# Moving the start addresses of weight tiles in SBUF: F panels by 64 bytes, down and gate panels by a table

## The chip, the cores and the metric

One core of one Trainium2 chip runs the whole kernel in one launch. The metric is the device time in microseconds of one execution. Of the kernel before there are three runs: 1002.62, 1002.34 and 1002.54 us, median 1002.54.

## The reference, cut to what matters

The reference takes x (256 tokens by 1024 features, float32) through two layers of one kind and then a block of another kind. Only the chain of products matters here; each has 1024 input features unless noted.

```
layer 0: h = x + mixer_ab(rmsnorm(x))           # stick-breaking attention and a gated recurrence, 3584 + 1024 columns
layer 1: h = h + mixer_c(rmsnorm(h))            # sliding-window attention, 1536 + 1024 columns
both:    h = h + conv_glu_ffn(rmsnorm(h))       # up 5632 columns, 3-tap convolution, silu(gate)*up, down 2816 -> 1024
         h = h + sigmoid(rmsnorm(h) @ ple_gate) * (p @ ple_proj)
block 2: proj = rmsnorm(h) @ w_in               # 9472 columns: three branches and three mixing gates
         y = sum over branches of (branch @ w_branch) * sigmoid(gate)
         out = rmsnorm(h + y @ w_out)
```

All products are of float32 data.

## The kernel before, in words

**Splitting.** TensorE is used in its float32r mode. Each operand is split in a high part (rounded to float32r) and a low part (the rest), and each product is three matmuls: high by high, high by low, low by high. The activations are in x_hi and x_lo or y_hi and y_lo (8 tiles of 128 features by 256 tokens each), in g_hi and g_lo (the FFN's gated features, and the branch outputs in block 2) or in pt_hi and pt_lo.

**Panels.** All weights are cut into 157 panels of 128 x 2048 floats (1 MB), in a fixed order (`PANELS`). SyncE loads panel n into one of three raw slots; ScalarE makes `w_hi` of it (L1211), VectorE makes `w_lo` (L1539, one panel is made by GpSimd, L734), both in rings of three slots (L369, L370); then TensorE multiplies. A load waits until `w_lo` of the panel three before is made (L632), and ScalarE waits until TensorE is done with the panel three before.

**Three kinds of panel**, each with its own order of matmuls in TensorE's function `panel`:
- F (67 panels, 48 matmuls each, L866): the weights are the operand that is loaded into the array (128 x 128) and the activations are streamed (256 columns). These are the two FFN up products (22 panels each: up0 with y, up1 with x), and fb, qb, qa, ka, mk, qc, gc, ga, gb2 and ub (23 panels, all with x).
- W (58 panels, 24 matmuls each, L841): the activations are loaded (128 x 128) and the weights are streamed (512 columns). Fourteen of them use y: kv, qs, wo1 and gate1. The mixing gates of block 2 are mc, mb and ma, four panels each.
- BT (32 panels, 24 matmuls each, L898, or L886 for the last panel of a branch): activations loaded, weights streamed (512 columns), four results at once. These are the FFN's down products (down0 and down1, 11 panels each), pp0, pp1 and the branch products brc, brb, bra.

TensorE loads the operand of the next matmul while the present one is streaming: in the trace each LDWEIGHTS begins together with the matmul before the one it is for.

**Addresses.** Tensors are placed by hand, in bytes of a partition. The first one is at 16512, that is 128 modulo 256. The `fixed` tensors (the raw, high and low slots, x_hi, x_lo, h, xn, whose place y_hi shares, ident, tri, vecs, small, g_hi and g_lo) follow each other in sizes that are multiples of 256 bytes; a slot of weights is 8192 bytes. Behind them, in regions that several stages share, come the others. All sizes there are multiples of 256 bytes but that of `relb` (32 x 16 floats, 64 bytes), which stands ahead of `buck`, y_lo and row_early (L435 to L438). So all operands of the products begin at 128 modulo 256 and y_lo begins at 192. Steps inside a tensor are 512, 1024, 2048 or 4096 bytes.

**Order.** All engines walk one list of steps, `SCHEDULE`, built by `schedule()`; each engine does its part of a step and waits on semaphores for the rest. Between the panels stand the attention steps, the turns (transposes) and, in up0 after its sixth panel, the small matmul of the bias step (L1073).

## Time and profile before

| | |
|---|---|
| median of three runs | 1002.54 us (1002.34 to 1002.62) |
| the profiled execution's own time | 1002.47 us |
| its span, first to last instruction | 1000.4 us |
| PE busy | 982.3 us, 98% (6186 matmuls) |
| PEld (weight loads) busy | 880.0 us, 88% |
| DVE / ACT / POOL busy | 674.2 / 573.8 / 135.9 us |
| mean granted clock of TensorE | 0.998 of full speed |
| DMA | 173.65 MB, mean 174 GB/s |

A matmul's recorded duration overlaps the next one's, so the durations say little of the pace. The pace is the distance from one start to the next: the time of a piece of the chain divided by its count of matmuls, or the difference of two starts in the timeline divided by the number of matmuls between them. The timeline rounds starts to 0.01 us.

### The profile page before, as it was taken

Reading aid. Unit: us, or ns where it says so; the run is one execution under the profiler, and the core shown is the slowest. Engines: PE = TensorE matmul, PEld = TensorE weight load, DVE = VectorE, ACT = ScalarE, POOL = GpSimd, SP = SyncE. Lnnn points to the kernel's source line nnn. Section 1 sums busy time; section 2 is a strip of 40 time slices with the busy share of each in tenths; the row PEclk is TensorE's granted clock in tenths of the full one; section 3 lists DMA queues with packets and bytes.
Section 4 is the critical chain, followed back from the end, with each engine's and each line's share of the span. In section 5 each row is a group of like instructions: output and inputs, shape, how many; then the busy total and the mean of one; then the engine's idle time right before and its main releaser. Section 6 shows DMA issues by size and latency. Waiting matters only on the chain.

```text
span 1000.4 us, 15440 instructions
## 1 busy us (share of the span) xinstructions
PE 982.3 (98%) x6186; PEld 880.0 (88%) x6186; DVE 674.2 (67%) x963; ACT 573.8 (57%) x801; POOL 135.9 (14%) x119
## 2 busy tenths in 40 slices
PE   8999999999999999999999999999999999999997
PEld 8988889999988888788999998888988889988886
DVE  5886477888863567876788886456564566854555
ACT  7747747566543576775756654356464465534433
POOL 5002202343310000000133331001000000000010
PEclk9999999999999999999999999999999999999999
DMA  9654266687555555336666655546645544456541
GB/s 295 199 168 126 85 166 178 194 245 200 173 208 178 163 206 169 127 116 170 188 171 191 187 172 208 175 161 206 211 128 169 168 155 140 146 192 209 175 170 55
DMA packets 159510, 173.65 MB, mean 174 GB/s; under 512 B 4110, under 2 KB 120320, under 8 KB 159440
## 3 DMA queue, kind: packets, MB, share of 16 engines
q1 hardware_dynamic: 157104, 167.00, 53.3%
q0 software_dynamic: 2160, 5.41, 1.7%
q8 instruction: 49, 0.80, 0.3%
q10 hardware_dynamic: 176, 0.27, 0.1%
q14 instruction: 21, 0.17, 0.1%
HBM read 171.59 MB, written 1.07 MB: 173 GB/s over the span
## 4 chain that ended last, share of the span: by engine, by line
PE 82%; DVE 7%; ACT 6%; issue 3%; DMA 1%; SPq 0%; POOL 0%; POOLq 0%; ACTq 0%; DVEq 0%
PE bank L866 31%; PE bank L841 28%; PE bank L898 16%; ACT w_hi L1211 2%; DVE w_lo L1539 2%; PE bank L886 2%; PE bank L926 1%; PE bank L1000 1%; ACT le L1321 1%; DMA w_raw<-in_ab_w_in 1%; DMA h<-in_x 1%; ACT L1321 1%; PE bank L946 0%; DVE x_lo L1553 0%; DVE le_s L1901 0%
## 5 line engine op out<-in xcount | busy, mean ns | idle before, releaser
L1539 DVE TENSOR_TENSOR w_lo<-w_raw,w_hi 128x2048 fp32r<-128x2048 f32 x154 | 352.0, 2289 | 188.6 <-ACT w_hi L1211 188.5
L1211 ACT ACTIVATE w_hi<-w_raw 128x2048 fp32r<-128x2048 f32 x155 | 296.2, 1914 | 243.4 <-PE bank L866 113.5
L866 PE MATMUL bank<-x_hi,w_hi 128*128 128x256 f32 x720 | 205.9, 286 | 0.8 <-DVE w_lo L1539 0.5
L866 PE MATMUL bank<-x_hi,w_lo 128*128 128x256 f32 x720 | 203.7, 283 | 0.0
L866 PE MATMUL bank<-x_lo,w_hi 128*128 128x256 f32 x720 | 203.7, 283 | 0.0
L841 PE MATMUL bank<-w_hi,x_hi 128*128 128x512 f32 x352 | 140.2, 398 | 3.2 <-DVE kaT L1695 2.2
L866 PEld LDWEIGHTS bank<-x_hi,w_hi 128*128 128x128 f32 x720 | 138.0, 192 | 2.4 <-DVE w_lo L1539 0.7
L866 PEld LDWEIGHTS bank<-x_lo,w_hi 128*128 128x128 f32 x720 | 138.1, 192 | 0.2
L866 PEld LDWEIGHTS bank<-x_hi,w_lo 128*128 128x128 f32 x720 | 138.0, 192 | 0.0
L841 PE MATMUL bank<-w_hi,x_lo 128*128 128x512 f32 x352 | 137.8, 391 | 0.0
L841 PE MATMUL bank<-w_lo,x_hi 128*128 128x512 f32 x352 | 137.6, 391 | 0.0
L694 POOL TENSOR_TENSOR gf<-sgate,cc 128x256 f32<-128x256 f32 x44 | 82.2, 1869 | 161.5 <-ACT sgate L1238 161.5
L866 PE MATMUL bank<-y_hi,w_hi 128*128 128x256 f32 x352 | 98.8, 281 | 0.1
L866 PE MATMUL bank<-y_hi,w_lo 128*128 128x256 f32 x352 | 98.4, 280 | 0.0
L866 PE MATMUL bank<-y_lo,w_hi 128*128 128x256 f32 x352 | 98.4, 279 | 0.0
L841 PEld LDWEIGHTS bank<-w_hi,x_hi 128*128 128x128 f32 x352 | 66.2, 188 | 18.2 <-DVE kaT L1695 2.6
L841 PEld LDWEIGHTS bank<-w_hi,x_lo 128*128 128x128 f32 x352 | 66.4, 189 | 14.2
L841 PEld LDWEIGHTS bank<-w_lo,x_hi 128*128 128x128 f32 x352 | 66.5, 189 | 13.2
L1648 DVE SCALAR_TENSOR_TENSOR cc<-conv_in,vecs,cc 128x254 f32<-128x254 f32 (+1 forms) x176 | 73.9, 482 | 0.0
L898 PE MATMUL bank<-w_hi,g_hi 128*128 128x512 f32 x216 | 66.7, 390 | 0.0
L898 PE MATMUL bank<-w_hi,g_lo 128*128 128x512 f32 x216 | 66.5, 389 | 0.0
L898 PE MATMUL bank<-w_lo,g_hi 128*128 128x512 f32 x216 | 66.5, 389 | 0.0
(353 smaller groups left out, 1461.4 us busy)
## 6 DMA issues: line engine op xcount, KB each, us to landing
w_raw<-in_ffn_up SPq DMA_DIRECT2D x88, 512.0 KB, 5.2
w_raw<-in_w_in SPq DMA_DIRECT2D x35, 1024.0 KB, 5.1
w_raw<-in_ffn_down SPq DMA_DIRECT2D x22, 1024.0 KB, 4.9
w_raw<-in_ab_w_in SPq DMA_DIRECT2D x13, 1024.0 KB, 5.2
w_raw<-in_ple_gate SPq DMA_DIRECT2D x8, 1024.0 KB, 5.1
w_raw<-in_c_w_in SPq DMA_DIRECT2D x6, 1024.0 KB, 5.4
w_raw<-in_ab_w_out SPq DMA_DIRECT2D x4, 1024.0 KB, 5.1
w_raw<-in_w_mem_kv SPq DMA_DIRECT2D x4, 1024.0 KB, 5.8
```

The lines of the kernel that those rows point to most:

```text
L694: pool.tensor_tensor(gf[i % 2][:, :], sgate[i % 2][:, :], cc[i % 3][:, 1, :], ALU.mult).then_inc(*mark("gated", ("gf", l, i)))
L841: mm = pe.matmul(bank[b][:, :], x[:, 4 * half + k, t * P:(t + 1) * P], wv[w][:, k, :], start=(half == 0 and k == 0 and m == 0), stop=(half ...
L866: mm = pe.matmul(bank[b][:, c * 256:c * 256 + 256], wv[w][:, k, c * P:(c + 1) * P], x[:, k, :], start=(k == 0 and m == 0 and not (first an ...
L886: mm = pe.matmul(bank[out_bank(t, half)][:, :], x[:, k0 + 2 * i + k, t * P:(t + 1) * P], wv[w][:, k, half * 512:half * 512 + 512], start=F ...
L898: mm = pe.matmul(bank[out_bank(t, half)][:, :], x[:, k0 + 2 * i + k, t * P:(t + 1) * P], wv[w][:, k, half * 512:half * 512 + 512], start=( ...
L926: mm = pe.transpose(bank[b][:, q * 256 + t * P:q * 256 + (t + 1) * P], src[:, t, kt * P:(kt + 1) * P], ident[:, :])
L1000: mm = pe.matmul(bank[b][:, o:o + 64], X[:, hd, t * P:(t + 1) * P], later(X[:, hd:hd + 1, t * P:(t + 1) * P], LEVELS[li])[:, 0, :, :], sta ...
L1211: act.activation(whi[n % RING][:, :], raw[n % RAW][:, :], ACT.Copy).then_inc(*mark("weights_hi", ("hi", n)))
L1321: act.activation(dst, src, ACT.Exp, scale=scale, bias=s_neg[:, c:c + 1], accum_out=s_sum[:, c:c + 1]).then_inc(*mark("exponentials", ("e", ...
L1539: dve.tensor_tensor(wlo[n % RING][:, :], raw[n % RAW][:, :], plain(whi[n % RING][:, :]), ALU.subtract).then_inc(*mark("weights_lo", ("lo", ...
L1648: dve.scalar_tensor_tensor(v, conv_ins[int(stage[-1])][i % 2][:, c, 0:T - d], vec("ffn_conv", int(stage[-1]), tap)(c * FT + i), v, ALU.mul ...
```

## The change

The high and low slots become 64 floats (256 bytes) longer, and a panel's weights begin `shift_of(n)` floats into its slot, the same in the high and the low slot, whichever of the three it is: 16 floats (64 bytes) for every F panel; for down and gate panels what a table says; 0 for all others. In the table the down products have one value for each group of three panels, and the two last panels of each product have 0.

| panels | bytes |
|---|---|
| down0, panels 0-2 / 3-5 / 6-8 | 16 / 32 / 48 |
| down1, panels 0-2 / 3-5 / 6-8 | 192 / 128 / 64 |
| mc / mb / ma, four panels each | 96 / 112 / 80 |

Beside that the region's next address is rounded so that y_lo begins at 128 modulo 256 like the others. To make room, `tri` moves from the fixed tensors to a region of the first layer, and `causal` to a part of `vecs` that held convolution weights. The raw slots stay where they are relative to each other. No instruction is added or removed.

```diff
--- before.py
+++ after.py
@@ -31,6 +31,8 @@
 FOURS = len(LEVELS)
 ORDER = [-1, FOURS] + list(range(FOURS))
 RAW, RING = 3, 3
+ROOM, F_SHIFT = 64, 16
+W_SHIFT = {("down0", 0): 4, ("down0", 1): 8, ("down0", 2): 12, ("down1", 0): 48, ("down1", 1): 32, ("down1", 2): 16, "mc": 24, "mb": 28, "ma": 20}
 WARM_UP = 12
 BIAS_AT = 6
 PIECES = {0: 4, 1: 2}
@@ -194,6 +196,12 @@
 def block_done(stage, block):
 
     return FIRST[stage] + (2 + block if stage in HALVES_FIRST else 2 * block + 1)
+
+
+def shift_of(n):
+
+    stage, i, _, kind, _ = PANELS[n]
+    return F_SHIFT if kind == "F" else W_SHIFT.get((stage, i // 3), 0) if kind == "BT" else W_SHIFT.get(stage, 0)
 
 
 WIDE_BLOCK = {}
@@ -366,14 +374,22 @@
             return t
 
         raw = [fixed(f"w_raw{i}", [P, 2048]) for i in range(RAW)]
-        whi = [fixed(f"w_hi{i}", [P, 2048], F32R) for i in range(RING)]
-        wlo = [fixed(f"w_lo{i}", [P, 2048], F32R) for i in range(RING)]
+        hi_room = [fixed(f"w_hi{i}", [P, 2048 + ROOM], F32R) for i in range(RING)]
+        lo_room = [fixed(f"w_lo{i}", [P, 2048 + ROOM], F32R) for i in range(RING)]
+
+        def w_hi(n):
+            a = shift_of(n)
+            return hi_room[n % RING][:, a:a + 2048]
+
+        def w_lo(n):
+            a = shift_of(n)
+            return lo_room[n % RING][:, a:a + 2048]
+
         XH, XL = (fixed(n, [P, KT, T], F32R) for n in ("x_hi", "x_lo"))
         h = fixed("h", [P, TT, D])
         xn_at = top[0]
         xn = fixed("xn", [P, TT, D])
         ident = fixed("ident", [P, P])
-        tri = fixed("tri", [P, P])
         vecs = fixed("vecs", [P, 5, P])
         small = fixed("small", [P, 320])
         g_at = top[0]
@@ -406,7 +422,7 @@
         sc_in, sc_over = g("sc_in", [P, HG_HEADS * TT, P]), g("sc_over", [P, HG_HEADS, P])
         exb = g("exb", [P, HG_HEADS, T])
         xs_buf = [r(f"xs{i}", [P, HG_HEADS, T]) for i in range(2)]
-        ones = g("ones", [P, P])
+        ones, tri = g("ones", [P, P]), r("tri", [P, P])
         heads = lambda x: x.rearrange("p (h t) -> p h t", h=HG_HEADS)
         four_q, four_k = heads(prod[:, :, :].rearrange("p t c -> p (t c)")), heads(on[:, :, :, :].rearrange("p t h c -> p (t h c)"))
         four_mid = prod[:, 0, 0:T].rearrange("p (n a) -> p n a", a=1)
@@ -433,6 +449,7 @@
         bias = r("bias", [P, SW_HEADS, T])
         brow = r("brow", [16, 3 * P])
         relb, buck = r("relb", [32, 16]), r("buck", [32, P])
+        r.at += (t_at - r.at) % 256
         YL = r("y_lo", [P, KT, T], F32R)
         YH = nc.alloc_sbuf_tensor_at("y_hi", [P, KT, T], F32R, offset=xn_at)
         row_early = r("row_early", [P, T])
@@ -463,7 +480,6 @@
         le, wT = r("le", [P, 2, 2, T]), r("wT", [P, 2, 2, T])
         va2, vb = r("va2", [P, TT, 768]), r("vb", [P, TT, 768])
         wsp, bsp = r("wsp", [P, GROUPS, P]), r("bsp", [P, GROUPS, P])
-        causal = r("causal", [P, T])
         r = Region(t_at, t_at + 4 * 3072)
         ubs, ga = r("ubs", [P, GROUPS, T]), r("ga", [P, MOBA_HEADS, T])
         r = Region(t_at + 4 * 3072, end)
@@ -502,6 +518,7 @@
         sw_tmp = [qkn[:, 0, 23, :], qkn[:, 0, 15, :]]
 
         vflat = vecs[:, :, :].rearrange("p a b -> p (a b)")
+        causal = vflat[:, 3 * P:3 * P + T]
 
         def vec(name, layer, *more):
             return lambda i: vflat[:, VEC[(name, layer, *more)] + i:VEC[(name, layer, *more)] + i + 1]
@@ -731,7 +748,7 @@
                     n = args[0]
                     pool.wait_ge(*at(("hi", n)))
                     for c in (slice(512 * q, 512 * q + 512) for q in range(4)):
-                        pool.tensor_tensor(wlo[n % RING][:, c], raw[n % RAW][:, c], plain(whi[n % RING][:, c]), ALU.subtract).then_inc(*mark("weights_lo_p", ("lo", n)))
+                        pool.tensor_tensor(w_lo(n)[:, c], raw[n % RAW][:, c], plain(w_hi(n)[:, c]), ALU.subtract).then_inc(*mark("weights_lo_p", ("lo", n)))
                 elif kind == "sb_scores":
                     i = args[0]
                     for r in range(2):
@@ -770,7 +787,7 @@
                     load(wsp_raw, io["w_spatial_2"][0].rearrange("g t s -> t g s"), "wsp")
                     load(bsp[:, :, :].rearrange("p g t -> p (g t)"),
                          bass.AP(tensor=io["b_spatial_2"].tensor, offset=0, ap=[[0, P], [1, GROUPS * P]]), "bsp")
-                    load(causal[:, :], io["c_causal"], "causal")
+                    load(causal, io["c_causal"], "causal")
                     load(small[:, 0:64], io["c_rope"], "rope")
                     pool.wait_ge(*at(("loaded", "wsp")))
                     pool.affine_select(out=wsp_raw, in_=wsp_raw, compare_op=ALU.is_ge, fill=0.0, base=0, pattern=[[0, GROUPS], [-1, P]], channel_multiplier=1).then_inc(*mark("spatial_masked", ("wspm",)))
@@ -808,7 +825,7 @@
 
                 stage, i, name, kind, where = PANELS[n]
                 xh, xl, k0, needs = XIN[stage]
-                wh, wl = whi[n % RING], wlo[n % RING]
+                wh, wl = w_hi(n), w_lo(n)
                 pieces = PIECES.get(n, 1)
                 pe.wait_ge(*at(("lo_piece", n, 0) if pieces > 1 else ("lo", n)))
 
@@ -825,7 +842,7 @@
                             turn(k, j)
                 if kind == "W":
                     block, half = where[2:]
-                    wv = [w[:, :].rearrange("p (k n) -> p k n", k=4) for w in (wh, wl)]
+                    wv = [w.rearrange("p (k n) -> p k n", k=4) for w in (wh, wl)]
                     for t in range(TT):
                         b = wide_bank(stage, block, t)
                         if half == 0:
@@ -849,7 +866,7 @@
                 elif kind == "F":
                     b = pb(n)
                     claim(b, ("ev", n))
-                    wv = [w[:, :].rearrange("p (k n) -> p k n", k=KT) for w in (wh, wl)]
+                    wv = [w.rearrange("p (k n) -> p k n", k=KT) for w in (wh, wl)]
                     first = i == 0
                     for c, k in [(c, k) for k in range(KT) for c in range(2)] if first else [(c, k) for c in range(2) for k in range(KT)]:
                         if c == 0 and first:
@@ -877,7 +894,7 @@
                         for t in range(TT):
                             for half in range(2):
                                 claim(out_bank(t, half), ("h", stage, t) if down else ("ym", stage[-1], 2 * t + half) if branch else ("ev", FIRST["gate" + stage[-1]] + 2 * half + 1))
-                    wv = [w[:, :].rearrange("p (k n) -> p k n", k=2) for w in (wh, wl)]
+                    wv = [w.rearrange("p (k n) -> p k n", k=2) for w in (wh, wl)]
                     if branch and last:
 
                         for t, half in [(t, half) for t in range(TT) for half in range(2)]:
@@ -1208,13 +1225,13 @@
                     act.wait_ge(*at(("raw", n)))
                     if n >= RING:
                         act.wait_ge(*at(("pe", n - RING)))
-                    act.activation(whi[n % RING][:, :], raw[n % RAW][:, :], ACT.Copy).then_inc(*mark("weights_hi", ("hi", n)))
+                    act.activation(w_hi(n), raw[n % RAW][:, :], ACT.Copy).then_inc(*mark("weights_hi", ("hi", n)))
 
             def split_piece(n, i):
 
                 c = slice(2048 // PIECES[n] * i, 2048 // PIECES[n] * (i + 1))
                 act.wait_ge(*at(("raw_half", i // 2) if n == 0 else ("raw", n)))
-                act.activation(whi[n % RING][:, c], raw[n % RAW][:, c], ACT.Copy).then_inc(*mark("weights_hi", ("hi_piece", n, i)))
+                act.activation(w_hi(n)[:, c], raw[n % RAW][:, c], ACT.Copy).then_inc(*mark("weights_hi", ("hi_piece", n, i)))
 
             act.dma_start(xn[0:2 * KT, 0, 0:P], io["mix_norm"].rearrange("l (a c) -> (l a) c", c=P)).then_inc(*mark("load_mix_gain", ("loaded", "mix_gain"), by=16))
 
@@ -1536,13 +1553,13 @@
             def split(n):
                 if n < len(PANELS) and n != POOL_SPLIT:
                     dve.wait_ge(*at(("hi", n)))
-                    dve.tensor_tensor(wlo[n % RING][:, :], raw[n % RAW][:, :], plain(whi[n % RING][:, :]), ALU.subtract).then_inc(*mark("weights_lo", ("lo", n)))
+                    dve.tensor_tensor(w_lo(n), raw[n % RAW][:, :], plain(w_hi(n)), ALU.subtract).then_inc(*mark("weights_lo", ("lo", n)))
 
             def split_piece(n, i):
 
                 c = slice(2048 // PIECES[n] * i, 2048 // PIECES[n] * (i + 1))
                 dve.wait_ge(*at(("hi_piece", n, i)))
-                dve.tensor_tensor(wlo[n % RING][:, c], raw[n % RAW][:, c], plain(whi[n % RING][:, c]), ALU.subtract).then_inc(*mark("weights_lo", ("lo_piece", n, i), ("lo", n)))
+                dve.tensor_tensor(w_lo(n)[:, c], raw[n % RAW][:, c], plain(w_hi(n)[:, c]), ALU.subtract).then_inc(*mark("weights_lo", ("lo_piece", n, i), ("lo", n)))
 
             def rest(src, gain, hi, lo, name, event, *first):
```

## Rows read from the trace of the kernel before

**Rows 1.** The page: busy shares, granted clock in 40 slices, the chain that ended last.
```profile
PE 982.3 (98%) x6186; PEld 880.0 (88%) x6186; DVE 674.2 (67%) x963; ACT 573.8 (57%) x801; POOL 135.9 (14%) x119
...
PEclk9999999999999999999999999999999999999999
...
PE 82%; DVE 7%; ACT 6%; issue 3%; DMA 1%; SPq 0%; POOL 0%; POOLq 0%; ACTq 0%; DVEq 0%
PE bank L866 31%; PE bank L841 28%; PE bank L898 16%; ACT w_hi L1211 2%; DVE w_lo L1539 2%; PE bank L886 2%; PE bank L926 1%; PE bank L1000 1%; ACT le L1321 1%; DMA w_raw<-in_ab_w_in 1%; DMA h<-in_x 1%; ACT L1321 1%; PE bank L946 0%; DVE x_lo L1553 0%; DVE le_s L1901 0%
```
**Rows 2.** The chain in order of time: start us, us, engine, output, line, count.
```profile
155.35 28.05 PE bank L866 x234
183.72 90.66 PE bank L866 x768
...
452.29 5.54 PE bank L841 x24
...
479.34 120.22 PE bank L866 x1002
600.00 65.31 PE bank L898 x288
...
894.34 21.76 PE bank L841 x96
```
**Rows 3.** Timeline of PE, first and second FFN: start us, us, instruction.
```profile
183.12 0.28 PE L866 MATMUL bank<-y_hi,w_lo 128*128 128x256 f32 x1
183.33 0.39 PE L1073 MATMUL bank<-buck,relb 32*16 32x128 f32 x2
...
249.84 0.28 PE L866 MATMUL bank<-y_hi,w_hi 128*128 128x256 f32 x1
...
250.90 0.28 PE L866 MATMUL bank<-y_hi,w_hi 128*128 128x256 f32 x1
...
539.76 0.28 PE L866 MATMUL bank<-x_lo,w_hi 128*128 128x256 f32 x1
...
540.84 0.28 PE L866 MATMUL bank<-x_lo,w_hi 128*128 128x256 f32 x1
```
**Rows 4.** Timeline of PE in the second PLE gate, the first and nineteenth start.
```profile
674.09 0.39 PE L841 MATMUL bank<-w_hi,y_hi 128*128 128x512 f32 x1
...
678.25 0.39 PE L841 MATMUL bank<-w_hi,y_hi 128*128 128x512 f32 x1
```
**Rows 5.** Tiles y_lo and w_lo: durations ns min/median/max, and who waited for w_lo.
```profile
L841 PE MATMUL bank<-w_hi,y_lo x112: 389/397/398, 365.8 to 690.7; 128*128 128x512 f32 x112
...
L1539 DVE TENSOR_TENSOR w_lo<-w_raw,w_hi x154: 2277/2291/2295, 19.1 to 980.0; 128x2048 fp32r<-128x2048 f32 x154
...
  PEld bank L866: 1.1, 2
  PE bank L866: 0.7, 2
```
**Rows 6.** Groups of PE by line and form: count, busy us, mean ns.
```profile
L866 PE MATMUL bank<-x_hi,w_hi 128*128 128x256 f32 x720 | 205.9, 286 | 0.8 <-DVE w_lo L1539 0.5 <-DVE w_lo L1545 0.2
...
L841 PE MATMUL bank<-w_hi,x_lo 128*128 128x512 f32 x352 | 137.8, 391 | 0.0
...
L866 PE MATMUL bank<-y_hi,w_hi 128*128 128x256 f32 x352 | 98.8, 281 | 0.1
...
L841 PE MATMUL bank<-w_hi,y_hi 128*128 128x512 f32 x112 | 44.6, 398 | 0.7 <-DVE y_lo L1553 0.7
```
**Rows 7.** Busy time of each engine in a stretch of the second FFN.
```profile
core 0: us, PE busy (x) PEld busy (x) DVE busy (x) ACT busy (x) POOL busy (x), PEclk, DMA share, GB/s
480.00:590.00 110.00, 110.00 (x919) 110.00 (x918) 90.95 (x132) 68.75 (x95) 35.35 (x18) 1.00 0.66 187
```
**Rows 8.** The page's DMA issues: count, KB each, us to landing.
```profile
w_raw<-in_ffn_up SPq DMA_DIRECT2D x88, 512.0 KB, 5.2
w_raw<-in_w_in SPq DMA_DIRECT2D x35, 1024.0 KB, 5.1
```

## The prediction

> **What bounds the kernel now.** First the page's busy shares and the granted clock: PE is busy 98% of the span, the next engine (DVE) 67%, and the clock stands at its upper level, 2.4 GHz, in all 40 slices [rows 1]. Then the chain that ended last: 82% PE, and three lines of weight products (L866, L841, L898) hold 75% of it [rows 1]. So the time is the number of matmuls times the distance from one start to the next; waits can give little. The distances come from the chain in order of time [rows 2]. L866 in the second FFN: 120.22 us for 1002 matmuls, 120.0 ns each. L898: 65.31/288 = 226.8. L841 in the last wide stages: 21.76/96 = 226.7. From 256 to 512 streamed columns the distance grows by 106.7 ns, 0.417 ns a column, one cycle at 2.4 GHz. What is left is 13.3 ns (32 cycles), the same for both widths. I call it the fixed part; 32 cycles on each matmul is what the change can reach.
>
> **Why addresses may matter.** All weight slots and all activations of the products start at the same place modulo 256 bytes, but for one buffer: `relb` has 64 bytes a partition, so y_lo, allocated behind it, lies 64 bytes further. That gives two natural experiments.
> - y_lo streamed (first FFN, L866, weights loaded). After 184 us, 90.66/768 = 118.0 ns [rows 2]; a look at ten starts gives 1.06/9 = 117.8 against 1.08/9 = 120.0 in the second FFN [rows 3]. Only one matmul in three streams y_lo, so three of them cost 353.3 instead of 360: 6.7 ns, 16 cycles. Before 183.3 us the same stage runs at 28.05/234 = 119.9 [rows 2], and it changes over just where one small matmul of the bias step stands between panels [rows 3]: the gain depends on how the streams were in step before.
> - y_lo loaded (wide stages of the sliding attention and second PLE gate, L841, weights streamed). 4.16/18 = 231.1 ns [rows 4], and 5.54/24 = 230.8 in a panel of the output product [rows 2], against 226.7: three cost 13.3 ns (32 cycles) more. The durations say the same, 397 ns where y_lo is the loaded operand [rows 5] against a mean of 391 for x_lo [rows 6].
>
> So the addresses of the two operands do change the distance, and with both signs.
>
> **The change, part by part.** No instruction, DMA or wait is added or taken; starts of tensors move. The tables `tri` and `causal` go to other places, loaded by the same DMAs at the same points of their queues, behind the same waits: nothing.
>
> *F panels, x inputs.* 720 x 3 = 2160 matmuls [rows 6] load weights that now lie 64 bytes after the streamed input. Not shown before: this pair in every matmul. From above the nearest row is the loaded y_lo, +13.3 ns a load; from below the whole fixed part, -13.3 ns. I take the streamed y_lo, since line, shape and stage kind are the same: one offset pair saves 6.7 ns and the two equal ones nothing. With all three offset it is 6.7 ns each: 113.3 ns. 2160 x 6.67 = -14.4 us. I choose this against the sign: there the streamed operand was the one further on, here the loaded one is, as in the L841 stages. My reason is that equal starts carry the fixed part everywhere (120.0, 226.7, 226.8), which looks like a collision at the moment when load and stream begin together, while in the L841 stages the loaded base also jumps from matmul to matmul, which the new layout doesn't do.
>
> *F panels, y inputs.* 352 x 3 = 1056 matmuls [rows 6] of the first FFN, now (234 x 119.9 + 768 x 118.0)/1002 = 118.5 ns. y_lo is aligned and the weights are offset, so 113.3: 1056 x 5.2 = -5.5 us.
>
> *y_lo aligned in the wide stages.* 112 x 3 = 336 matmuls [rows 6] get the addresses of the x stages: 231.1 to 226.7, 336 x 4.4 = -1.5 us. This term is the surest.
>
> *The table.* 18 down and 12 gate panels, 24 matmuls each: 720, all streaming the shifted weights. Six panels (64 and 192 bytes, 144 matmuls) are like the streamed y_lo: -6.7 ns, -1.0 us. The other 24 (16, 32, 48, 80, 96, 112, 128 bytes) have no row near them; I take zero. Bounds for all 720: the fixed part gone or doubled, 9.6 us either way.
>
> *Cover.* If a panel of the FFN takes 48 x 113.3 = 5.44 us instead of 5.76, DVE's 90.95 us in 110 [rows 7] becomes 88% of the time, and ACT's 68.75 66%: they still fit. The split of a panel takes DVE 2.29 us [rows 5], and PE waited for it 1.8 us in all [rows 5]. A panel's load lands 5.2 us after issue [rows 8] with three raw slots. What would be late next is DVE, from about 100 ns a matmul. Shifted writes of ACT and DVE I cost at nothing: they lie beside PE.
>
> **Sum.** -14.4 - 5.5 - 1.5 - 1.0 = -22.4 us, against the profiled execution's 1002.47 us (span 1000.4 and 2.07 around it): 980.1. The median of the runs is 0.07 us higher, no difference here. I forecast 980.
>
> The skill bears on this against the change. The Trainium skill, TensorE: Matmul & The Clock Gate, section on the steps of a matmul, says that PE reads the streamed operand and the loaded one through two independent ports, and that loading "doesn't steal SBUF read bandwidth from the running matmul". By that no start address would matter, and the sum would be zero; the trace disagrees, with 117.8 and 120.0, and 231.1 and 226.7, for the same work. That is the third rival below. The same page's section on the issue gap has N/2.4 + 2.5 ns, 109.2 for 256 columns, where the row has 120.0; an estimate by it would put the floor at 968 us.
>
> **The rivals.**
> 1. *The sign decides (slower).* Loaded 64 bytes after streamed costs 13.3 ns, as the wide y stages show, and now every F matmul has that pair: 133.3 ns. 2160 x 13.3 = +28.8, 1056 x (133.3 - 118.5) = +15.6, less 1.5: 1045. For it: it is the only row with this sign. Against: that row has jumping bases and 512 columns. The point from which it decides: any F distance above 120.3 ns makes the kernel slower.
> 2. *Small gain.* An offset anywhere only brings the pace of the settled first FFN, 117.8 to 118.0: 2160 x 2.1 = -4.5, 1056 x 0.6 = -0.6, less 1.5, table about 0: 996. For it: it is what a row shows outright.
> 3. *Nothing.* F stays at or returns to 120.0: 1056 x 1.5 = +1.6, -1.5: 1002.6. Ports that don't collide would give this.
> 4. *The table costs.* F as in 3, and starts that are no multiple of 64 bytes cost 6.7 to 13.3 ns on 720 matmuls: +4.8 to +9.6, 1007 to 1012.
> 5. *The whole fixed part of F goes.* -13.3 x 2160 - 11.8 x 1056 - 1.5 us: 960.
>
> **How the numbers follow.** Forecast (about 980, with the table's bounds 970 to 990) 0.38; small gain 0.22; all of it gone 0.03; nothing 0.08; the table costs 0.12; the sign decides 0.17. A measurement of this kernel can tell about 0.2%, 2 us, from no change. Faster: 0.38 + 0.22 + 0.03 = 0.63; same 0.08; slower 0.12 + 0.17 = 0.29. The range leaves out 960 and 1045, 0.20 together: from 970 (forecast with the table at its best bound) to 1013 (nothing in F, the table at its worst). The forecast's own range is 970 to 990.
>
> **What would show it.** L866 distances in the second FFN: 113.3 (forecast), 117.8 (rival 2), 120.0 (3), 133.3 (1). L841 in the y stages: 226.7, and the 397 ns of y_lo down to 389 to 391. The down panels fall into three groups of three, each with its own distance, beside two unshifted ones at 226.7; likewise the gate panels of the last block. DVE's and ACT's busy time should stay within 1%. I am wrong if F goes above 120.3 ns, if the distance follows the sign and not the offset, or if PE begins to wait for w_lo.

## The result and the profile after

The kernel after takes 994.39 us (median; 993.91 to 999.28) where the kernel before, on the same chips, takes 1002.30: a ratio of 0.9931, interval 0.9915 to 0.9948. It is faster by 8 us, where 22 had been forecast.

The profiled execution of after is the longest of its seven, 999.28 us; the other six lie between 993.91 and 994.85. So the profile shows 3.2 of those 8 us, and the other 5 need an explanation of their own (they get one below). Lines have moved: L866 is now L883, L841 is L858, L898 is L915.

The page of after: busy time, granted clock, and the chain that ended last, by line.

```profile
PE 978.4 (98%) x6186; PEld 873.8 (88%) x6186; DVE 674.4 (68%) x963; ACT 573.8 (58%) x801; POOL 134.0 (13%) x119
...
PEclk9999999999999999999999999999999999999999
...
PE bank L883 30%; PE bank L858 28%; PE bank L915 16%; PE bank L903 2%; DVE w_lo L1556 2%; ACT w_hi L1228 2%; PE bank L943 1%; PE bank L1017 1%; DMA w_raw<-in_ab_w_in 1%; ACT le L1338 1%; ACT L1338 1%; PE bank L963 0%; DVE x_lo L1570 0%; PE bank L986 0%; DVE le_s L1918 0%
```

Against [rows 1] nothing has changed place: PE is busy 98% of the span, the clock is at its upper level in all 40 slices (one dip of a few us doesn't show in them; it is told of at the end), and three lines of weight products hold 74% of the chain. DVE (674.4 us) and ACT (573.8 us) are busy as long as before. So the difference again lies in the distance from one matmul to the next.

The chain of after in order of time (start us, us, engine, output, line, count):

```profile
154.41 26.55 PE bank L883 x234
181.28 90.66 PE bank L883 x768
272.38 66.65 PE bank L915 x288
...
477.62 118.02 PE bank L883 x1002
596.08 66.46 PE bank L915 x288
...
837.31 16.96 PE bank L883 x144
856.96 22.42 PE bank L858 x96
...
890.30 22.18 PE bank L858 x96
...
928.84 22.19 PE bank L858 x96
```

Divide each by its count. First FFN: 113.5 ns up to the bias step, then 118.0; before, 119.9 and 118.0 [rows 2]. Second FFN: 118.02/1002 = 117.8 ns (120.0 before). The three ub panels (837.31): 117.8. Down products: 66.65/288 = 231.4 and 66.46/288 = 230.8 ns, 226.8 before [rows 2]. Mixing gates mc, mb, ma: 22.42, 22.18 and 22.19 us for 96, that is 233.5, 231.0 and 231.1 ns, 21.76 (226.7) for mb before [rows 2]. One product became faster, the other slower.

Two starts nine matmuls apart, in the timeline of PE in the first FFN, ahead of the bias step and behind it:

```profile
169.92 0.28 PE L883 MATMUL bank<-y_hi,w_hi 128*128 128x256 f32 x1
...
170.94 0.28 PE L883 MATMUL bank<-y_hi,w_hi 128*128 128x256 f32 x1
...
249.87 0.28 PE L883 MATMUL bank<-y_hi,w_hi 128*128 128x256 f32 x1
...
250.93 0.28 PE L883 MATMUL bank<-y_hi,w_hi 128*128 128x256 f32 x1
```

1.02/9 = 113.3 ns and 1.06/9 = 117.8 ns: the same instructions on the same addresses at two paces. Panel by panel (the median of the sums of three distances, a third of it) every F panel of after runs at one of these two, 13 of the 67 at 113.3 to 114.7 and 54 at 117.7 to 118.0.

The tile y_lo of after as the loaded operand (count, ns min/median/max):

```profile
L858 PE MATMUL bank<-w_hi,y_lo x112: 388/389/398, 364.7 to 687.5; 128*128 128x512 f32 x112
```

Who waited for w_lo in after (us, times):

```profile
  PE bank L883: 2.0, 1
```

y_lo's products take 389 ns, where [rows 5] had 397. PE's wait for w_lo rose from 0.7 to 2.0 us.

**What the profiled execution adds up to.** First FFN -1.5 us (117.21 for 118.71), second FFN -2.2, wide stages with y -1.2 (four stages, the sum of their distances), the table +3.9 (down 1.34 + 1.15, gates 0.6 + 0.4 + 0.4), the 15 F panels of layer 1 and the last block -2.3, the start up to the first FFN -0.9 (155.35 to 154.41). That is -4.2; the span went down by 3.1, so 1.1 us more went into pauses that I didn't follow. The 0.9 us of the start needn't be F's pace alone: a short dip of the clock lies elsewhere in the two executions (last section).

### The profile page after: what moved, and what is told of

It reads as the page before. It is cut to its first block, busy times and chain, and to the rows that moved or that the text cites. A ratio compares the mean times of both kernels' runs of the same rounds, so it can differ in the third digit from the quotient of the medians.

```text
span 997.3 us, 15440 instructions
## 1 busy us (share of the span) xinstructions
PE 978.4 (98%) x6186; PEld 873.8 (88%) x6186; DVE 674.4 (68%) x963; ACT 573.8 (58%) x801; POOL 134.0 (13%) x119
## 4 chain that ended last, share of the span: by engine, by line
PE 83%; DVE 7%; ACT 6%; issue 3%; DMA 1%; POOL 0%; POOLq 0%; ACTq 0%; DVEq 0%
PE bank L883 30%; PE bank L858 28%; PE bank L915 16%; PE bank L903 2%; DVE w_lo L1556 2%; ACT w_hi L1228 2%; PE bank L943 1%; PE bank L1017 1%; DMA w_raw<-in_ab_w_in 1%; ACT le L1338 1%; ACT L1338 1%; PE bank L963 0%; DVE x_lo L1570 0%; PE bank L986 0%; DVE le_s L1918 0%
## 5 line engine op out<-in xcount | busy, mean ns | idle before, releaser
L883 PE MATMUL bank<-x_hi,w_hi 128*128 128x256 f32 x720 | 204.8, 284 | 2.1 <-DVE w_lo L1556 2.0
L883 PE MATMUL bank<-x_lo,w_hi 128*128 128x256 f32 x720 | 202.4, 281 | 0.0
L883 PE MATMUL bank<-x_hi,w_lo 128*128 128x256 f32 x720 | 202.4, 281 | 0.0
L858 PE MATMUL bank<-w_hi,x_hi 128*128 128x512 f32 x352 | 140.1, 398 | 2.6 <-DVE kaT L1712 1.5
L883 PEld LDWEIGHTS bank<-x_hi,w_hi 128*128 128x128 f32 x720 | 136.3, 189 | 3.7 <-DVE w_lo L1556 2.2
L858 PE MATMUL bank<-w_lo,x_hi 128*128 128x512 f32 x352 | 137.7, 391 | 0.0
L883 PEld LDWEIGHTS bank<-x_hi,w_lo 128*128 128x128 f32 x720 | 137.6, 191 | 0.0
L858 PE MATMUL bank<-w_hi,x_lo 128*128 128x512 f32 x352 | 137.5, 391 | 0.0
L883 PEld LDWEIGHTS bank<-x_lo,w_hi 128*128 128x128 f32 x720 | 136.4, 189 | 0.2
L883 PE MATMUL bank<-y_hi,w_hi 128*128 128x256 f32 x352 | 98.9, 281 | 0.1
L883 PE MATMUL bank<-y_lo,w_hi 128*128 128x256 f32 x352 | 98.5, 280 | 0.0
L883 PE MATMUL bank<-y_hi,w_lo 128*128 128x256 f32 x352 | 98.5, 280 | 0.0
L858 PEld LDWEIGHTS bank<-w_hi,x_hi 128*128 128x128 f32 x352 | 66.1, 188 | 18.2 <-DVE kaT L1712 2.0
L858 PEld LDWEIGHTS bank<-w_hi,x_lo 128*128 128x128 f32 x352 | 66.0, 188 | 14.5
L858 PEld LDWEIGHTS bank<-w_lo,x_hi 128*128 128x128 f32 x352 | 66.1, 188 | 13.4
L883 PEld LDWEIGHTS bank<-y_hi,w_hi 128*128 128x128 f32 x352 | 67.2, 191 | 0.5 <-DVE y_lo L1570 0.3
L915 PE MATMUL bank<-w_hi,g_hi 128*128 128x512 f32 x216 | 67.5, 394 | 0.0
L915 PE MATMUL bank<-w_lo,g_hi 128*128 128x512 f32 x216 | 67.4, 393 | 0.0
```

The lines of the kernel that those rows point to most:

```text
L858: mm = pe.matmul(bank[b][:, :], x[:, 4 * half + k, t * P:(t + 1) * P], wv[w][:, k, :], start=(half == 0 and k == 0 and m == 0), stop=(half ...
L883: mm = pe.matmul(bank[b][:, c * 256:c * 256 + 256], wv[w][:, k, c * P:(c + 1) * P], x[:, k, :], start=(k == 0 and m == 0 and not (first an ...
L915: mm = pe.matmul(bank[out_bank(t, half)][:, :], x[:, k0 + 2 * i + k, t * P:(t + 1) * P], wv[w][:, k, half * 512:half * 512 + 512], start=( ...
```

## The experiments

Each kernel is the kernel after with the edit that is shown, unless the text says otherwise.

| kernel | what it is | us, median | ratio to before |
|---|---|---|---|
| f_only | F 64 bytes, no table | 991.39 (991.06 to 992.42) | 0.9894 (0.9879 to 0.9909) |
| y_only | only y_lo aligned | 1003.12 (1001.51 to 1003.86) | 1.0010 (1.0001 to 1.0019) |
| f_minus | F 192 bytes, no table | 993.27 (988.15 to 994.07) | 0.9895 (0.9865 to 0.9925) |
| base_plus | f_only, all tensors 64 bytes on | 991.77 | one run |
| after_again | the kernel after, once more | 993.88 | one run |
| f_kick | f_only, three panels at 80 bytes | 994.21 (992.04 to 994.56) | 0.9917 (0.9903 to 0.9930) |
| bias_late | f_only, bias step later | 989.51 | one run |
| scan | a start of its own for each panel | 1000.58 | one run |
| scan_fine | the same, near 64 and 192 bytes | 997.26 | one run |
| f_52 | F 52 bytes, no table | 987.78 (986.55 to 988.69) | 0.9853 (0.9840 to 0.9867) |
| f_76 | F 76 bytes, no table | 1000.47 (998.89 to 1000.89) | 0.9979 (0.9970 to 0.9988) |
| f_mix | F 52 or 76 bytes by stage | 985.28 (984.98 to 986.97) | 0.9843 (0.9828 to 0.9858) |
| halves | f_only, gates in matmuls of 256 | 992.87 | one run |

### The parts of the change

**f_only**: F panels at 64 bytes, the table empty.

```diff
-W_SHIFT = {("down0", 0): 4, ("down0", 1): 8, ("down0", 2): 12, ("down1", 0): 48, ("down1", 1): 32, ("down1", 2): 16, "mc": 24, "mb": 28, "ma": 20}
+W_SHIFT = {}
```

> Only the F panels are offset (64 bytes); the table is empty, y_lo is aligned. Theory: the table only costs. In the changed kernel's profile its 720 matmuls run at 228.9 to 233.3 ns instead of 226.7, some 3.9 us in all, so this version takes about 990.5 us, with all down and mixing-gate panels back at 226.7 ns. F panels run at one of two paces, 113.3 or 117.8 ns, changing only at pauses. Rival (the table's groups were harmless and their longer distances come from elsewhere, such as the slower writes of ScalarE): 994 us and L915 still above 226.7.

The chain of f_only:

```profile
154.26 27.56 PE bank L883 x234
182.14 87.27 PE bank L883 x768
269.85 65.33 PE bank L915 x288
...
473.76 118.02 PE bank L883 x1002
592.22 65.32 PE bank L915 x288
...
851.94 21.81 PE bank L858 x96
```

Both down products are back at 226.8 ns, and mc (851.94) is at 227.2. The median is 3.0 us below that of after, against the 3.9 us of the table's pieces. So the table only cost. The F pieces show something else: here the first FFN is slow up to the bias step (27.56/234 = 117.8) and fast behind it (87.27/768 = 113.6), the reverse of after.

**y_only**: neither F nor the table shifted; only y_lo lies like the others.

```diff
-ROOM, F_SHIFT = 64, 16
+ROOM, F_SHIFT = 64, 0
```

with `W_SHIFT = {}` as above.

> Only y_lo is aligned; all weights start at 0. Theory (relative start decides): wide y stages at 226.7 instead of 231.1 (-1.5 us), first FFN at 120.0 instead of 118.5 (+1.6 us), so 1002 to 1003 us. Rival (aligning alone gives part of the gain): 1000 us or below, with F under 120 ns.

```profile
154.52 28.06 PE bank L883 x234
182.90 92.35 PE bank L883 x768
...
479.75 120.22 PE bank L883 x1002
```

That is the chain of y_only: 119.9, 120.2 and 120.0 ns. With all starts equal every F panel runs at 120.0, also behind the bias step, where [rows 2] had 118.0: +1.7 us, which takes away what the wide stages with y gained. The gain of the change comes from F's offset, 991.39 - 1003.12 = -11.7 us, against which stand the table's 3.0 us and the 0.8 of y_only (1003.12 - 1002.30). The three add up to the 7.9 us of the change by the way they are formed; the sum is no test of its own.

### Is it the sign, or the place in memory?

**f_minus**: F panels 192 bytes in, which is 64 bytes ahead of the next streamed start modulo 256.

```diff
-ROOM, F_SHIFT = 64, 16
+ROOM, F_SHIFT = 64, 48
```

with `W_SHIFT = {}`.

> F panels' weights 192 bytes in, that is 64 bytes behind the streamed input instead of ahead, no table, y_lo aligned. Theory A (only that the two starts differ by 64 bytes counts, not which is ahead): same paces as with 64 bytes, 990 to 992 us. Theory B (the sign counts, as streamed and loaded operand are not alike): other paces; the streamed y_lo of before, the only row with this sign, saved 16 cycles in one of three, so 113.3 ns throughout and 983 to 985 us if each offset pair saves as much, or up to 120 ns and 1002 us if not.

The same two paces as in f_only, 113.3 (18 panels) and 117.8 (49), and 993.27 us. The sign doesn't decide. That 192 bytes ahead is the same as 64 behind takes a period of 256 bytes for granted; no run tests it by itself, but the slots are 8448 bytes long, so their starts alternate modulo 512, and the paces don't alternate from panel to panel. Its executions spread over 6 us (988.15 to 994.07), more than those of any other kernel here.

**base_plus**: f_only with every tensor that is placed by hand 64 bytes further on.

```diff
-        top = [16512]
+        top = [16576]
```

> The version with only the F panels offset, but all tensors of the kernel begin 64 bytes later (the first at 16576 instead of 16512). Theory (only the difference between the streamed and the loaded operand's start counts): W and BT panels at 226.7 ns, F at 113.3 or 117.8, 988 to 993 us. Rival (the place itself counts, modulo 256): other distances, F back at 120.0 or W and BT above 226.7.

991.77 us, the F panels again at 113.3 and 117.8 only, the down panels and mixing gates at 226.7. So what counts is how the starts stand to each other, not where they are, as far as one shift of 64 bytes shows it.

### The two rhythms

**after_again**: the kernel after, unchanged.

> The changed kernel once more, unchanged. Its profiled run took 999.3 us and its other six 994.3. Theory (two rhythms, fixed anew at the pauses): the time difference of one execution to the next lies in F panels alone, in whole stretches at 113.3 or 117.8 ns; if this execution takes about 994 us, some 20 more panels run at 113.3 ns than in the first profile. Rival (the 5 us come from elsewhere, such as the clock or DMA): the same paces in each F panel as in the first profile, and longer waits.

The chain of after_again:

```profile
180.65 90.66 PE bank L883 x768
...
476.68 113.59 PE bank L883 x1002
```

113.59 us for the second FFN, where the profiled execution of after has 118.02, with the same program. These 4.4 us are most of the 5.4 between the two executions (993.88 and 999.28). So an execution can take one of two rhythms in a stage and stays in it for over a thousand matmuls: 113.4 ns (with the pauses between panels) or 117.8.

**f_kick**: three single panels at 80 bytes, to see whether another offset throws PE out of its rhythm.

```diff
+KICK = {("up0", 1): 20, ("up0", 7): 20, ("up1", 2): 20}
...
-    return F_SHIFT if kind == "F" else W_SHIFT.get((stage, i // 3), 0) if kind == "BT" else W_SHIFT.get(stage, 0)
+    return KICK.get((stage, i), F_SHIFT) if kind == "F" else 0
```

> The version with only the F panels offset, but one panel early in each FFN's up product (the second and, behind the bias matmul, the eighth of the first FFN, the third of the second FFN) lies 80 bytes in. In the run in which every panel had its own start, all four panels at 64 bytes that were entered from another offset, without a pause, ran at 113.3 ns. Theory (two rhythms for the same addresses, kept until something breaks step; a panel at another offset brings PE into the fast one): both up products run at 113.3 ns behind these panels; against the version without them that saves 0.9 us (four panels before the bias matmul) + 4.1 us (19 panels of the second FFN) and costs 0.8 us: 987 us. Rival (the rhythm is a matter of chance at every change): no difference beyond 1 us from 991.4, and the two stages at 117.8 or 113.3 as it falls.

```profile
182.39 90.71 PE bank L884 x768
...
477.19 113.86 PE bank L884 x1002
```

That is its chain. The shifted panel itself goes at 118.7 ns, and after it the rhythm is the one from before: slow in the first FFN (90.71/768 = 118.1, where after_again without a shifted panel has 90.66), fast in the second (113.86 against 113.59; 48 x 5.4 ns = 0.26 for the one panel). Panel 1 of up0 says nothing: behind panel 0 the pace changes in after_again too. The theory that a panel at another offset brings PE into the fast rhythm fell, with its 987 us; the median is 994.21, 2.8 us above f_only's, and the profiled execution, 992.04, doesn't show why.

**bias_late**: the small matmul of the bias step comes after panel 14 instead of 6.

```diff
-BIAS_AT = 6
+BIAS_AT = 14
```

with `W_SHIFT = {}`.

> 64 bytes as before, but the bias matmul stands behind 14 panels of the first FFN instead of 6. In each of six profiles the first FFN's rhythm changed just at this matmul. Theory (a rhythm is kept until something breaks step): the first FFN changes its pace, if at all, at panel 14 and no more at panel 6. Rival (the pace depends on the panel or on what the other engines do then): it changes at panel 6 again.

```profile
154.94 70.07 PE bank L883 x618
225.32 45.44 PE bank L883 x384
...
475.03 113.59 PE bank L883 x1002
```

The chain of bias_late: 70.07/618 = 113.4 ns up to the step at its new place, 45.44/384 = 118.3 behind it. The change of pace moved with the foreign matmul. In the kernels in which all F panels have the same start the rhythm changes inside an FFN at two places only, at that matmul and behind the first panel, where PE pauses; elsewhere it may be another behind each pause of PE. What a pause or a foreign matmul does to it isn't in the program's hands as far as these runs go.

### The other offsets

**scan** and **scan_fine**: each panel of the FFNs (in scan those of the mixing gates too) has a start of its own.

```diff
-    return F_SHIFT if kind == "F" else W_SHIFT.get((stage, i // 3), 0) if kind == "BT" else W_SHIFT.get(stage, 0)
+    return SCAN[stage][i] if stage in SCAN else F_SHIFT if kind == "F" else 0
```

> Every panel of both FFN up products, both down products and the mixing gates has a start of its own: up0 and up1 take 0 to 240 bytes in steps of 16 in two different orders, with a few starts of 4, 8, 68, 72 and 132 bytes; the down and gate panels 4 to 248 bytes. The time says nothing, the distance within each panel does. Theory A (the difference modulo 256 bytes counts in 64-byte blocks): paces of F fall into plateaus of 64 bytes with 0 the slowest at 120.0, and for the streamed weights 0 is the best at 226.7 ns. Theory B (any difference will do): every F panel but 0 runs at 113 to 118 ns. Rival C (starts off a 64-byte boundary cost an extra line): 16, 32 and 48 bytes are slower than 0 in F too, as they were in the down panels (232 to 233 ns).

The timeline of scan in the second FFN: first and last start of 48 steps in the panel at 64 bytes, then the same in the panel at 112 bytes.

```profile
494.78 0.28 PE L889 MATMUL bank<-x_hi,w_hi 128*128 128x256 f32 x1
...
500.23 0.28 PE L889 MATMUL bank<-x_hi,w_hi 128*128 128x256 f32 x1
...
511.63 0.28 PE L889 MATMUL bank<-x_hi,w_hi 128*128 128x256 f32 x1
...
517.39 0.28 PE L889 MATMUL bank<-x_hi,w_hi 128*128 128x256 f32 x1
```

5.45/48 = 113.5 ns and 5.76/48 = 120.0 ns. Read so, panel by panel (ns; more values where more panels had the offset):

| bytes modulo 256 | F, weights loaded, 256 columns streamed | down and gates, weights streamed, 512 columns |
|---|---|---|
| 0 | 120.0 | 226.7 |
| 4 / 8 / 12 | 118.3 / 115.6, 115.8 / 116.6 | 8: 233 |
| 16 / 32 / 48 | 118.4 / 118.3 / 117.8 | 231.6 / 233 / 230 to 233 |
| 20 / 24 / 28 / 36 / 40 / 44 | 120.0 / 122.0 / 116.8 / 120.0 / 119.3 / 118.0 | not tried |
| 52 / 56, 60 | 113.3, 113.3 / 117.8, 119.6 | not tried |
| 64 | 113.3 or 117.7 | 229 |
| 68, 72 | 118.3 | not tried |
| 76 / 80 | 113.3 / 118.7 | 80: 231 |
| 96 | 117.3, 118.8, 120.1 | 233.3 |
| 112 / 128 | 120.0 / 118.8 | 231.1 / 232.2 |
| 132 to 176 | 118.2 to 120.0 | 233 to 234 |
| 180 to 188 / 196 to 204 / 212, 216 | 118.0 to 118.4 / 116.7 to 120.0 / 117.4, 119.8 | not tried |
| 192 | 113.3 or 117.8 | 233.4 |
| 208 / 224 | 116.7 / 116.7, 117.8 | 234.5 / 233 |
| 240 / 248 | 119.8 / not tried | 236.5 / 235.4 |

Two results. Offsets in F are no worse than equal starts, with one exception of size (24 bytes, 122 ns), and only 52, 64, 76 and 192 bytes reached 113.3. At 96 and 224 bytes, too, panels differ in pace. For streamed weights equal starts are the best of all; each of the 17 other starts costs 2.2 to 9.8 ns.

> Each panel of the two up products with a start of its own again, now in steps of 4 bytes around 64 and 192 and below 64. Theory (64 and 192 are sharp best points, 16 cycles above the streaming time at 113.3 ns): every start 4 bytes beside them is slower, 115 to 119 ns, as 68 and 72 bytes were (118.3). Rival (the 115.8 ns at 8 bytes shows a second valley): some start between 4 and 60 bytes comes to 113.3 ns or below. The panels at 64 and 192 bytes, entered from another offset, run at 113.3 in most cases.

scan_fine found the fast pace at 52 bytes (two panels of two) and at 76 (one of one), while 64 had it once and the slow one twice, and 192 once and three times the slow one. In scan the four panels at 64 that were entered from another offset without a pause had all been fast. So in these two runs panels with the same start go at both paces within one FFN, with only other offsets between them: a stretch of other offsets can change the rhythm as well, though f_kick's single panels didn't. That asked for whole kernels.

**f_52** and **f_76**: all F panels at one of the two.

```diff
-ROOM, F_SHIFT = 64, 16
+ROOM, F_SHIFT = 64, 13
```

(19 in f_76), with `W_SHIFT = {}`.

> F panels' weights 52 bytes in instead of 64, nothing else. In the finer run both panels at 52 bytes ran at 113.3 ns, one in each FFN, while panels at 64 did so in one of three. Theory (at 52 bytes there is only the fast rhythm): all F panels at 113.3 to 113.5 ns; against the 992.4 us of the profiled execution with 64 bytes, where 41 panels ran at 117.8, 41 x 48 x 4.4 ns = 8.7 us less, 984 us, and executions within 0.5 us of each other. Rival (52 bytes has two rhythms as well, and was lucky twice): 991 us with a spread of several us and stretches at a slower pace.

> F panels' weights 76 bytes in. One panel at 76 bytes ran at 113.3 ns. Theory (52 and 76, 12 bytes to either side of 64, behave alike): all F panels at 113.3 ns, 984 us. Rival (one panel of luck): 990 us or more, with panels at 117.8 to 119 ns.

The chain of f_52:

```profile
182.16 87.25 PE bank L883 x768
...
473.49 113.61 PE bank L883 x1002
...
827.66 17.29 PE bank L883 x144
```

and that of f_76:

```profile
183.45 92.36 PE bank L883 x768
...
479.86 120.24 PE bank L883 x1002
...
840.92 16.35 PE bank L883 x144
```

Both theories (984 us, all panels fast) fell: f_52 takes 987.78 us and f_76 1000.47. These offsets too have two rhythms, 113.3 and 120.0. They fall otherwise: f_52 is fast in both FFNs (113.6, 113.4) and slow in ten other panels (the ub ones, 17.29/144 = 120.1); f_76 is slow in both FFNs (120.3, 120.0) and in the first three F panels of the last block, and fast in its last ten (the ub ones, 16.35/144 = 113.5).

**f_mix**: for each stage the offset that had been fast in it.

```diff
-ROOM, F_SHIFT = 64, 16
+ROOM, F_SHIFT = 64, 19
+W_SHIFT = {}
+F_STAGE = {"up0": 13, "up1": 13, "mk": 13, "qc": 13, "gc": 13}
...
-    return F_SHIFT if kind == "F" else W_SHIFT.get((stage, i // 3), 0) if kind == "BT" else W_SHIFT.get(stage, 0)
+    return F_STAGE.get(stage, F_SHIFT) if kind == "F" else 0
```

> The best of what the profiles show, put together: 52 bytes for up0, up1, mk, qc and gc, 76 bytes for the other F panels, 0 for all streamed weights. With 52 bytes 10 panels (four at the start, six in the last block) ran at 120.0 ns, and with 76 bytes nine of these ran at 113.3. Theory (the rhythm follows from the addresses and the pause before a stretch, and repeats from run to run where these are the same): all F panels at 113.3 but one or two, 10 x 48 x 6.7 ns = 3.2 us less than with 52 bytes alone, 984.5 us. Rival (a change before a stretch shifts its pauses, and the rhythms fall anew): 987 to 989 us.

```profile
153.88 26.57 PE bank L884 x234
180.77 87.25 PE bank L884 x768
...
472.11 113.61 PE bank L884 x1002
...
825.65 16.35 PE bank L884 x144
```

All four F pieces of its chain are at 113.4 to 113.6 ns, and 65 of the 67 F panels at 113.3. 985.28 us, ratio 0.9843 (0.9828 to 0.9858): this version beats both kernels, after by 9 us.

### Is it the loaded weights, or the width?

**halves**: f_only, and each matmul of 512 columns in the twelve mixing gate panels is done as two of 256, with the weights 0 (mc), 64 (mb) and 192 bytes (ma) in.

```diff
-W_SHIFT = {("down0", 0): 4, ("down0", 1): 8, ("down0", 2): 12, ("down1", 0): 48, ("down1", 1): 32, ("down1", 2): 16, "mc": 24, "mb": 28, "ma": 20}
+W_SHIFT = {"mc": 0, "mb": 16, "ma": 48}
...
+                                if stage in ("mc", "mb", "ma"):
+                                    for c in range(2):
+                                        mm = pe.matmul(bank[b][:, 256 * c:256 * c + 256], x[:, 4 * half + k, t * P:(t + 1) * P], wv[w][:, k, 256 * c:256 * c + 256],
+                                                       start=(half == 0 and k == 0 and m == 0 and c == 0), stop=(half == 1 and k == 3 and m == 2), skip_group_check=True)
+                                    continue
```

> The twelve mixing-gate panels do each matmul of 512 streamed columns as two of 256, the same operand loaded for each; mc has its weights at 0, mb at 64, ma at 192 bytes, F panels at 64. Question: why is 0 the best start for the streamed weights and the worst for the F panels? Theory (the number of columns: the fast rhythm costs 17 cycles for 16 columns, 113.3 ns for 256 and 226.7 for 512, and the stream of 512 has it at equal starts, while the stream of 256 falls into the slow one): mc goes to 120.0 ns a half, mb and ma to 113.3 or 117.8. Rival (which operand is the weights, or the place in the kernel): mc stays at 113.3 a half, mb and ma become slower than that, about 115 to 117, as their 512-column forms at these starts (229 to 233 ns) were.

```profile
849.06 23.03 PE bank L860 x192
...
883.00 22.61 PE bank L860 x192
...
921.98 22.61 PE bank L860 x192
```

Its chain, mc, mb and ma in turn: 119.9, 117.8, 117.8 ns for 192 matmuls each. The same products in the same stages, streamed from the same tiles, behave like F as soon as 256 columns are streamed: equal starts are slow, 64 and 192 bytes faster. The width decides, not which of the operands is the weights, as far as these three starts show it.

## Where the prediction failed, and what in it was right

The miss is 14.5 us, 22.4 against 7.9, and it lies in two terms above all. By the prediction's own prices the steps from kernel to kernel are: y_lo aligned alone +0.1 us (1.6 - 1.5), F's offset beside it -21.4 (3216 x 6.67), the table -1.0. Measured are +0.8, -11.7 and +3.0. The step that failed most is the price of F's offset, 6.7 ns on every matmul: the runs show two rhythms at each of the four offsets that reach 113.3 ns, and in after most panels took the slower one, 117.8 ns.

**What bounds the kernel.** Right. The differences that could be placed are distances of PE, but for 0.9 us ahead of the first FFN; DVE and ACT are as busy as before.

**The fixed part.** This step failed too, and the table's term hangs on it: "13.3 ns (32 cycles), the same for both widths ... 32 cycles on each matmul is what the change can reach". The paces allow another split. 113.33 ns is 272 cycles at 2.4 GHz and 226.67 ns is 544: 17 cycles for 16 streamed columns in both. So a matmul of 512 columns was at that floor already, and one of 256 at 120.0 (288 cycles) stood 16 cycles above it, not 32. That no start made the 512 columns faster (18 starts tried) and that the halved gates fell to 120.0 and 117.8 is what the runs show; that 17/16 is the floor of any start stays argued, as it is only the lowest pace seen.

**F with x and y, -19.9 us.** Right in part: starts apart do shorten the distance, and the pace 113.3 exists. Wrong was the price, "one offset pair saves 6.7 ns and the two equal ones nothing. With all three offset it is 6.7 ns each: 113.3 ns". Prices of pairs don't add up: with one pair in three offset (before, settled first FFN) and with all three (after, the same matmuls) the pace of the chain is the same 118.0, and 117.8 within the panels. Nor does the saving lie with the offset pair: between 200 and 270 us of before the distance to the next start is 117.6 ns for y_hi with w_hi, 117.4 for y_lo with w_hi and 118.3 for y_hi with w_lo. In after 13 of 67 panels had 113.3, in after_again 38, in f_only 26. Measured, F brought 11.7 us (f_only against y_only). The pace of the settled first FFN, rival 2's 117.8, is the second rhythm of the same addresses. The timelines [rows 3] had shown both sides of this, a stage that changes its pace at a foreign matmul and keeps the new one; I read it as a story of y_lo alone. With nearly all panels fast (f_mix) it is 17.8 us against y_only, and by its own row 3216 x 6.67 = 21.4 would be due.

**Where the rest of f_mix's gain stays.** The eight F panels of the first stage should give 2.6 us. The chain of f_mix starts the first FFN at 153.88 us, that of y_only, at 120.0 ns, at 154.52. Over all kernels the start lies between 153.44 and 155.65 us and doesn't go by the paces. It goes rather by where the clock dipped (last section): 154.94 to 155.65 in the eight kernels, before among them, that have a dip between 65.5 and 71 us, 153.51 to 154.41 in the four that have it between 41 and 46.2, 153.44 to 154.52 in the three that have none. The rest is waiting: in f_mix PE waits 2.0 us for w_lo, at about 40 us, and 2.7 us for kaT (a tile of the first attention), at 66 us; in before 0.7 and 2.2. "PE begins to wait for w_lo" was among what would make me wrong, and in this one place the wait grew. That the faster F panels make it isn't shown: y_only, at 120.0 ns throughout, waits 1.7 us, and f_minus 0.7.

**y_lo in the wide stages, -1.5 us.** Right as a term: gate1's panels went from 231.1 to 226.7 ns, the durations from 397 to 389, -1.2 us by the sum of the four stages. But y_only shows that it needs F's offset beside it: alignment takes the first FFN's 118.0 away, so for itself it brings nothing (1.0010).

**The table, -1.0 us.** Wrong in sign: +3.9 us by its pieces, +3.0 by the medians. "Six panels (64 and 192 bytes) are like the streamed y_lo" took the row of a stream of 256 columns for panels of 512; they take 229 and 233 ns. The nearest row was the other one, L841 with loaded y_lo at 231.1: 512 columns and unequal starts. Rival 4 came near this, with its F part wrong; its price, 6.7 to 13.3 ns, is above the 2.2 to 6.7 measured in after, and multiples of 64 bytes cost too (2.2 ns at 64, over 5 at 128 and 192), which it had free.

**The rivals.** The sign (1045 us) fell with after itself, where no F panel is above 118.0, and f_minus has the same paces. "Nothing" fell with F's 117.8 at worst. Rival 2's 996 came nearest to 994.39, in part by accident: it had all F panels at the slow rhythm and no cost of the table. For the profiled execution it is close to the truth: 996 + 3.9 = 999.9, measured 999.28. The range (970 to 1013) held and the kernel did get faster, by a good third of what was forecast.

**The two ports.** The Trainium skill, TensorE: Matmul & The Clock Gate, section on the steps of a matmul, has two independent ports and a loading that steals no read bandwidth. The runs disagree: 120.0 and 113.3 ns, and 226.7 and 233.4, differ in nothing but the start of one operand. By the Trainium skill, the same page's section on the issue gap, 256 columns take N/2.4 + 2.5 = 109.2 ns, which it gives for a matmul by itself; no F panel of any run here came below 113.3.

**Still open.** What in the chip keeps the two rhythms, why 52, 64, 76 and 192 bytes reach the fast one and their neighbours 56 and 60 don't, and what chooses it at a pause. I didn't try other widths, shifts of the activations instead of the weights, or unequal shifts of w_hi and w_lo. The paces of every kernel come from one profile each (after from two), so how often a rhythm falls one way isn't known.

## What to carry to other kernels

Where PE is busy all the time, take its pace from distances of starts, for each stage and each shape, before costing a change: a pace of 120.0 ns for 256 columns in float32r had 6.7 ns in it that the start addresses could give back, one of 226.7 for 512 had nothing at any of the 17 other starts. Don't carry an effect of alignment from one width to another; try it alone, one kernel for each part, since here one part gained 11.7 us and another lost 3. And where the same instructions show two paces in one trace, the gain is a range from the start, and a single profile may show either end.

## What was not expected of the hardware

- **Two rhythms on the same addresses**: 113.3 and 117.8 ns at 64 and 192 bytes, 113.3 and 120.0 at 52 and 76, kept for up to 1002 matmuls, changed at pauses, by one foreign matmul and by panels at other offsets. They make executions of one program differ by 5.4 us (999.28 and 993.88).
- **The clock, and the 16 cycles that go with it.** In the profiled execution of after PE stood idle for 2.0 us behind w_lo (the wait above), and a moment later, at 42.7 us, the granted clock fell to one half, 1.2 GHz, and came back at 46.2. The windows of PE (stretch, us, busy and matmuls, granted clock, DMA share, GB/s), and two starts seven matmuls apart within it:

```profile
40.00:42.00 2.00, 0.45 (x3) 1.00 0.00 0
42.00:44.00 2.00, 2.00 (x15) 0.69 0.58 131
44.00:46.00 2.00, 2.00 (x11) 0.50 1.04 404
46.00:48.00 2.00, 2.00 (x19) 0.96 1.01 353
```

```profile
43.07 0.42 PE L883 MATMUL bank<-x_hi,w_lo 128*128 128x256 f32 x1
...
44.57 0.41 PE L883 MATMUL bank<-x_hi,w_hi 128*128 128x256 f32 x1
```

  1.50/7 = 214 ns for 256 columns; 256 cycles at 1.2 GHz are 213.3. At the lower level a column takes a cycle and nothing comes on top, neither 16 nor 32 cycles. So the extra time isn't a number of PE's own cycles; something that keeps its own pace, and is just too slow for 2.4 GHz, would look like that (argued, not tested). The dip cost some 1.6 us: its 16 matmuls would have taken 1.8 us at the upper level and took 3.4.

  The kernel before has the same dip, only later, at 67.4 to 70.8 us, behind a wait of 2.2 us for kaT:

```profile
66.00:68.00 2.00, 2.00 (x8) 0.85 0.00 0
68.00:70.00 2.00, 2.00 (x6) 0.50 0.27 42
```

  There a matmul of 512 columns takes 426.6 ns, again a cycle a column. So the dip is no price of the change. It comes at 41 to 43 us in after, after_again, f_only and scan, at 65.5 to 67.5 in before and seven experiments, and not at all (before the last instructions) in y_only, f_mix and halves. The length of the wait ahead doesn't settle it: f_76 waits 2.7 us for w_lo, longer than any, and has its dip only at 67 us, and f_mix, with 2.0 and 2.7 us, has none. By the starts of the first FFN above, its place is worth a microsecond or so there; no kernel tests it alone.
